# A hybrid decoder step on one core: the first norm moved behind its products, running sums taken on TensorE in split halves

## Chip, cores and metric

The kernel runs on one core of a Trainium2 chip. The metric is the device time of one execution in microseconds (us), lower is better, given as the median of several runs.

## The reference, cut to what matters

One step of a two-layer decoder is applied to 1024 prompt tokens and 8 sample tokens (1032 columns in all), with a model width of 1024. Only the start of the even layer is touched by the change:

```
hp = rmsnorm(xp, g_mix[l])                       # x * rsqrt(mean(x*x)+eps) * g
rq, rk, rv, rg, sq, sk, sv = split(h @ w_in)     # 28 tiles of 128 output features
# stick-breaking attention, per head of sq, sk, sv:
z = q @ k.T * hd**-0.5 + bias
log_1m = where(mask, log_sigmoid(-z), 0)         # -softplus(z)
after = reverse_cumsum(log_1m) - log_1m
a = where(mask, exp(log_sigmoid(z) + after), 0);  out = a @ v
# retention, per head: q, k = rotary(rq), rotary(rk); chunks of 128 tokens
ret_out = silu(rg) * head_layernorm(o, gn_g)
```

## The kernel before

Activations lie with features on the 128 partitions and the 1032 tokens in the free dimension: `X` has eight chunks of 128x1032. A product is run in full precision as three one-pass matmuls on rounded halves (`three`, line 435): `Wh*Hh + Wh*Hl + Wl*Hh`, each in three groups of 344 columns, so one chunk of the contraction is nine matmuls (`chunk`, L439) and a tile of 128 output features is eight chunks. GpSimd splits each 512 KB weight tile into `Wh` and `Wl` (L410, L412) when the tile two before it is done. SyncE queues the loads.

**Start.** SyncE loads the first quarter of x (1032 KB, two chunks), the constants (778 KB), the parameters (356 KB), the selectors (32 KB), the rest of x, then the weights. ScalarE squares each chunk, VectorE sums the squares (L1298 `acc`), TensorE adds over the partitions (`norm_sum`, L502), ScalarE takes the root, VectorE the reciprocal of all 1032 columns (L1326), and only then VectorE forms each normalised chunk `hf`, ScalarE its high half and VectorE its low half. The products wait for these. `first_pair` (line 468) runs two tiles together: chunks 0 to 3 of the first, then chunk k of the first beside chunk k-4 of the second. A third tile follows; ScalarE evacuates all three from PSUM.

Later norms are already in a deferred form (`DEFERRED`): the halves are made of x times its gain, the sum of squares runs beside the products (`high_of_x`, `low_of_x`, `group_sum` L465, `roots`, `reciprocals` L1378), and the reciprocal root is multiplied in where the product is evacuated.

**Stick-breaking, four heads.** The scores of a head are cut into 12 units of a key block of 128 and up to 512 queries; the widths are 128, 256, 384, 512, 512, 512, 512, 512, then 128, 256, 384, 512. Units go in pairs, six groups g per head. In each group TensorE runs, in this order: two score products of the next pair (L537), two chunks of the next head's products, the sums of the first unit (L547, L551), one chunk, the sums of the second unit, one chunk, the value products of the pair before (L560). So 24 chunks, three tiles, are spread over a head. Per unit VectorE scales the scores out of PSUM (L1409), ScalarE takes Abs, Exp and Ln, VectorE makes the softplus `sp`, and the cumulative sum over keys is two fp32 matmuls: a triangle times `sp`, and ones times a running sum `rr` that VectorE keeps (`later`, two buffers, cleared by a memset). VectorE subtracts the sum from the score (`exponent`), ScalarE takes Exp (`aa`). Banks 3 and 4 of PSUM hold scores, bank 5 the sums, 6 and 7 the values. ScalarE evacuates the next head's three tiles (`next_product`).

**Retention, four heads.** The tile of the gate `rg` is evacuated with Silu; rotary rows `cs` are loaded when stick-breaking has ended; the cached pages of the samples are streamed through two buffers by SyncE, each released by its consumer. The values are transposed and copied to `vt` by ScalarE. At the end of a head VectorE takes a reciprocal, and ScalarE evacuates the next gate after the last product with the old one (`r_c`).

Of the kernel before, what the change touches and what calls it, by code (L numbers as in the profile page):

```python
# [90 lines left out]
def build(nc, x_in, mem_in, wts, memw, cons, rope, selc, par, stc, stf0, stf1, stret,  # L91
          cache_k, cache_v, cmk, cmv, ptab,
          y, o_sbk, o_sbv, o_retp, o_rets, o_cvp, o_cvs, o_ffn0, o_ffn1, o_st0, o_st1, o_mk, o_mv):
    with ExitStack() as ctx:
# [25 lines left out]
        def sem(name):  # L120
# [26 lines left out]
        DEFERRED = (1, 2, 4, 5)  # L147
        n_at = [sum(3 if k in DEFERRED else 1 for k in range(nk)) for nk in range(7)]
        hf_at = {0: 0, 3: KC, 6: 2 * KC}
# [11 lines left out]
        rt, _ = layout([("cs", [P, 2, N]), ("rg", [P, N]),  # L161
# [8 lines left out]
        rt.update(layout([("rst", [P, N])], where["kt"])[0])  # L170

# [113 lines left out]
        LATER = {u: n for n, u in enumerate(u for u, (_, j, _, _) in enumerate(UNITS) if j)}  # L285
        NLATER = len(LATER)

# [6 lines left out]
        def _(sp):  # L294
# [26 lines left out]
            load_x(0)  # L321
            load(con[:, :], cons, ld_con)
            load(prm[:, :], par, ld_con)
            load(sel[:, :, :], selc, ld_con)
            for c in range(1, KC // 2):
                load_x(c)
            for j in range(2):
                weight(j, j, first=True)
            weights(2, T_RET + 6)

            ended(sp, E_SB)
            load(rt["cs"][:, :, :], rope, ss("ld_rope"))
# [68 lines left out]
        def _(pool):  # L401
# [13 lines left out]
            pool.wait_ge(ld_con, 48)  # L415
# [16 lines left out]
        def _(pe):  # L432
# [26 lines left out]
            def group_sum(nk, g):  # L459

                if g < 2:
                    pe.wait_ge(ss("n_acc"), KC * (nk + 1))
                else:
                    pe.wait_ge(ss("n_rt"), n_at[nk] + 1)
                mm(ps[:, 6 + g % 2, 0:GN], ones, dn["acc_d"][:, g * GN:(g + 1) * GN], start=True,  # L465
                   stop=True).then_inc(ss("n_sum"), 1)

            def first_pair(t, ready, freed=None, act_h=HA, nk=None):
# [44 lines left out]
            pe.wait_ge(ld_con, 48)  # L513
            norm_sum(0)

            first_pair(T_SB, split_ready(0))
            pe.wait_ge(ss("sb_ev"), 1)
            tile(T_SB + 2, 0, 0)
            for i in range(0, 2):
                for hh in range(2):  # L520
# [3 lines left out]
                    pe.wait_ge(ss("sb_ev"), 3 * h + 3)  # L524
                    if hh:
# [14 lines left out]
                    def sums(u):  # L540

                        half, j, q0, w = UNITS[u]
                        lone = j == 4 * half + 3
                        pe.wait_ge(ss("sb_sp"), NU * h + (u + 1))
                        if u >= 1 or hh:
# [385 lines left out]
        def _(act):  # L931
# [11 lines left out]
            def fixed():  # L943

                act.wait_ge(ld_con, 48)
# [21 lines left out]
            def high_of_x(nk, freed, gcol, act_h):  # L967

                for c in range(KC):
                    act.wait_ge(set_free[c % 2], freed + c // 2 + 2)  # L970
# [5 lines left out]
            def roots(nk):  # L976

                for g in range(GRP):
                    act.wait_ge(ss("n_sum"), n_at[nk] + g + 1)
                    fn(dn["rst_d"][:, g * GN:(g + 1) * GN], ps[:, 6 + g % 2, 0:GN], ACT.Sqrt, ss("n_rt"),  # L980
                       scale=1.0 / D, bias=eps)

            act.wait_ge(ld_con, 48)
            for c in range(KC):
                act.wait_ge(ld_x[c // 2], 16)
                square(0, c)
            norm(0)

            def sb_evacuate(j, hh, s, done):

                act.wait_ge(tile_done, done)
                fn(grp(sb[f"{'kvq'[j]}{hh}"][:, :]), pset(s), ACT.Copy, ss("sb_ev"))

            for j in range(3):
                sb_evacuate(j, 0, j % 2, T_SB + j + 1)
            for i in range(0, 2):
                for hh in range(2):
# [7 lines left out]
                    def front(g):  # L1005

                        for u in (2 * g, 2 * g + 1):
                            w = UNITS[u][3]
                            act.wait_ge(ss("sb_zs"), NU * h + (u + 1))
                            if u >= 4 or hh:  # L1010
                                act.wait_ge(ss("sb_sp"), NU * h + (u - 3))
# [1080 lines left out]
```

## Time and profile before

| | us |
|---|---|
| median of 3 runs | 3418.16 (3417.29 to 3421.23) |
| the profiled execution, its own time | 3422.02 |
| its span, first to last instruction | 3420.2 |
| PE busy in the span | 3210.9 (94%) |
| DVE busy | 1859.5 (54%) |
| ACT busy | 748.5 (22%) |
| POOL busy | 788.6 (23%) |

The engines are PE (TensorE matmuls), PEld (weight loads into TensorE), DVE (VectorE), ACT (ScalarE), POOL (GpSimd) and SP (SyncE). Busy shares are over the whole span; what counts for the change is the first fifth of it, up to about 683 us.

### The profile page before, as it was taken

How to read it: one execution, taken by the hardware profiler on the slowest of the kernel's cores; microseconds unless marked ns; L12 is line 12 of the kernel's file. 1: busy time of each engine (PE TensorE's matmuls, PEld its weight loads, DVE VectorE, ACT ScalarE, POOL GpSimd, SP SyncE). 2: the span in 40 equal slices, each digit the busy share in tenths (PEclk: the TensorE clock that was granted, in tenths of full speed). 3: DMA queues.
4: the chain of work that ended last, by engine and by line, in shares of the span. 5: the costliest groups of instructions: out<-in, count | busy, mean ns of one | idle time of the engine just before them, and what ended most of it. 6: DMA issues, size and time to landing. Idle time of an engine off the chain costs nothing.

```text
span 3420.2 us, 45029 instructions
## 1 busy us (share of the span) xinstructions
PE 3210.9 (94%) x19126; PEld 2953.8 (86%) x19126; DVE 1859.5 (54%) x2789; ACT 748.5 (22%) x1029; POOL 788.6 (23%) x424
## 2 busy tenths in 40 slices
PE   5999999499989999999998899799999999999996
PEld 4777888399769999999998788499679999999996
DVE  5444565643434654455546799852345554555456
ACT  3656222220031211111112322320032211111111
POOL 2111211033004233333333000123003332323331
PEclk9999999699999999999999999899999999999998
DMA  3011344422701111111112010012701111111111
GB/s 119 32 38 38 106 145 154 130 99 73 295 28 48 50 44 50 44 50 44 50 44 62 25 37 26 26 38 75 320 7 48 50 44 50 44 50 44 50 44 69
DMA packets 83643, 238.16 MB, mean 70 GB/s; under 512 B 15722, under 2 KB 20714, under 8 KB 81522
## 3 DMA queue, kind: packets, MB, share of 16 engines
q1 hardware_dynamic: 74962, 217.96, 19.4%
q10 hardware_dynamic: 8480, 17.32, 1.4%
q8 instruction: 151, 2.47, 0.3%
q14 instruction: 50, 0.41, 0.0%
HBM read 217.93 MB, written 17.32 MB: 69 GB/s over the span
## 4 chain that ended last, share of the span: by engine, by line
PE 85%; DVE 9%; DMA 2%; ACT 1%; issue 1%; SPq 1%; ACTq 0%; DVEq 0%
PE ps L439 69%; PE ps L897 2%; PE ps L815 2%; PE ps L738 2%; PE ps L726 2%; PE ps L792 1%; DVE tls L1306 1%; DVE X L1298 1%; DMA pg<-in_cv 1%; PE ps L560 1%; PE ps L547 1%; PE ps L551 1%; PE ps L537 1%; PE ps L502 1%; DVE Gl L1298 1%
## 5 line engine op out<-in xcount | busy, mean ns | idle before, releaser
L439 PE MATMUL ps<-Hh,Wh 128*128 128x344 f32 x3552 | 792.3, 332 | 53.3 <-DVE Hl L1298 45.4
L410 POOL CAST Wh<-wraw 128x1024 fp32r<-128x1024 f32 x210 | 233.4, 1111 | 2565.0 <-PE ps L439 2531.9
L439 PE MATMUL ps<-Hl,Wh 128*128 128x344 f32 x3552 | 758.4, 322 | 0.0
L439 PE MATMUL ps<-Hh,Wl 128*128 128x344 f32 x3552 | 754.8, 321 | 0.0
L439 PEld LDWEIGHTS ps<-Hh,Wh 128*128 128x128 f32 x3552 | 604.0, 190 | 92.6 <-issue 75.8
L439 PEld LDWEIGHTS ps<-Hl,Wh 128*128 128x128 f32 x3552 | 605.6, 190 | 0.0
L439 PEld LDWEIGHTS ps<-Hh,Wl 128*128 128x128 f32 x3552 | 596.8, 189 | 0.0
L412 POOL TENSOR_TENSOR Wl<-wraw,Wh 128x1024 fp32r<-128x1024 f32 x210 | 555.1, 2643 | 16.8
L1298 DVE TENSOR_TENSOR X<-ps,X 128x1032 f32<-128x1032 f32 x200 | 244.4, 1230 | 296.6 <-PE ps L439 296.6
L1298 DVE TENSOR_TENSOR ub<-ps,rst_d 128x1032 f32<-128x1032 f32 x88 | 108.5, 1233 | 424.8 <-PE ps L439 241.7
L1302 DVE SCALAR_TENSOR_TENSOR cb<-ub,fp,cb 128x1024 f32<-128x1024 f32 x176 | 275.7, 1566 | 93.4 <-ACT cb L939 93.4
L939 ACT ACTIVATE cb<-ub,fp 128x1032 f32<-128x1032 f32 x88 | 110.1, 1252 | 967.5 <-DVE ub L1298 967.5
L439 PE MATMUL ps<-Gh,Wh 128*128 128x344 f32 x1056 | 225.7, 322 | 4.0 <-DVE X L1298 4.0
L439 PE MATMUL ps<-Gl,Wh 128*128 128x344 f32 x1056 | 224.2, 320 | 0.0
L439 PE MATMUL ps<-Gh,Wl 128*128 128x344 f32 x1056 | 224.2, 320 | 0.0
L439 PEld LDWEIGHTS ps<-Gh,Wh 128*128 128x128 f32 x1056 | 176.3, 188 | 9.7 <-DVE X L1298 9.7
L439 PEld LDWEIGHTS ps<-Gl,Wh 128*128 128x128 f32 x1056 | 178.2, 188 | 0.0
L439 PEld LDWEIGHTS ps<-Gh,Wl 128*128 128x128 f32 x1056 | 177.2, 188 | 0.0
L439 PE MATMUL ps<-Hh_s,Wh 128*128 128x344 f32 x768 | 164.7, 323 | 0.0
L439 PE MATMUL ps<-Hl_s,Wh 128*128 128x344 f32 x768 | 162.8, 320 | 0.0
L439 PE MATMUL ps<-Hh_s,Wl 128*128 128x344 f32 x768 | 162.1, 319 | 0.0
L1302 DVE SCALAR_TENSOR_TENSOR ca<-uu,cpar,ca 128x512 f32<-128x512 f32 (+1 forms) x232 | 155.0, 744 | 0.0
(234 smaller groups left out, 3320.1 us busy)
## 6 DMA issues: line engine op xcount, KB each, us to landing
wraw<-in_wts SPq DMA_DIRECT2D x224, 512.0 KB, 3.5
pg<-in_ck SPq DMA_DIRECT2D x64, 256.0 KB, 2.8
pg<-in_cv SPq DMA_DIRECT2D x64, 256.0 KB, 2.8
cc<-in_cmk SPq DMA_DIRECT2D x16, 1024.0 KB, 9.8
cc<-in_cmv SPq DMA_DIRECT2D x16, 1024.0 KB, 9.6
X<-in_x SPq DMA_DIRECT2D x8, 1032.0 KB, 7.2
mwa<-in_memw SPq DMA_DIRECT2D x16, 512.0 KB, 7.5
mwb<-in_memw SPq DMA_DIRECT2D x16, 512.0 KB, 7.6
```

Of the source, the lines that this page charges most:

```text
L410: pool.tensor_copy(Wh[:, j, :], wraw[:, j, :]).then_inc(w_hi, 1)
L412: pool.tensor_tensor(Wl[:, j, :], wraw[:, j, :], Wh[:, j, :].bitcast(F32), ALU.subtract).then_inc(w_split, 1)
L439: ins = mm(o, w[:, wcol[0], wcol[1]:wcol[1] + P], r, start=first and a == 0, stop=last and a == 2)
L502: ins = mm(ps[:, 3 * s + g, 0:GN], ones, src[:, g * GN:(g + 1) * GN], start=True, stop=True)
L537: mm(ps[:, 3 + u % 2, 0:w], k_[:, j * P:(j + 1) * P], q[:, q0:q0 + w], start=True, stop=True).then_inc(ss("sb_z"), 1)
L726: ins = mm(ps[:, mk_bank(c), 0:MEM], mws[c % 4][:, k * P:(k + 1) * P], nmem["memT"][:, k, :], start=k == 0, stop=k == KC - 1)
L738: ins = mm(ps[:, 6 - 2 * half + m, :], nmem["memT"][:, 2 * kk + k, m * P:(m + 1) * P], mws[t % 4][:, k * 512:(k + 1) * 512], start=(kk == ...
L815: ins = mm(ps[:, 6 + dc, :], cr["mv"][:, m, (2 * hx + dc) * P:(2 * hx + dc + 1) * P], at["pT"][:, u % 2, m, :], start=m == 0, stop=m == MT ...
L897: ins = mm(ps[:, 6 + c % 2, :], cf["dg"][:, n, :], cf["us2"][:, n:n + TH], start=n == 0, stop=n == W_PE - 1)
L939: ins = act.activation(out, in_, f, **kw)
L1298: ins = dve.tensor_tensor(out, a, b, op)
L1302: ins = dve.scalar_tensor_tensor(out=out, in0=in0, scalar=scalar, in1=in1, op0=op0, op1=op1)
```

## The change

Three things are altered. The first norm takes the deferred form: products run on x times its gain, and the reciprocal root `rst0` (kept where chunk 3 of x was) is multiplied in at each evacuation, which moves from ScalarE to VectorE. For retention it is multiplied into the rotary rows once, inside head 1, into the values by a per-token scale (`rtok`, made by nine one-column matmuls), and into the gate by VectorE before Silu. The loads are put in another order, in pieces of one, two, two and three chunks, each weight between them. And the running sum `rr` goes: PSUM bank 5 keeps the sum across units, to which each unit adds its own triangle (`own`), after the rest of the unit before (`next`, ones minus triangle), each in two one-pass matmuls on the high and low half of the softplus, with three slots for the halves.

```
-        DEFERRED = (1, 2, 4, 5)
+        DEFERRED = (0, 1, 2, 4, 5)
...
-                        ("sp", [P, 2, 512]), ("rr", [P, 2, 512]), ("ea", [P, 4, 512]),
-                        ("aa", [P, 2, 512])], hd_end)
+                        ("sph", [P, 3, 512], F32R), ("spl", [P, 3, 512], F32R),
+                        ("ea", [P, 4, 512]), ("aa", [P, 2, 512]),
+                        ("own", [P, P], F32R), ("next", [P, P], F32R)], hd_end)
...
+        rst0 = C[:, 3, :]
+        rope0 = C[:, 0:2, :]
...
# SyncE
+            first_x(0, 0, 1)
+            load(prm[:, :], par, ss("ld_rope"))
+            weight(0, 0, first=True)
+            first_x(1, 1, 3)
+            weight(1, 1, first=True)
+            first_x(2, 3, 5)
+            first_x(3, 5, KC)
             load(con[:, :], cons, ld_con)
             load(sel[:, :, :], selc, ld_con)
+            weights(2, 4)
+            sp.wait_ge(ss("n_acc"), KC)
+            load(rope0, rope, ss("ld_rope"))
+            weights(4, T_RET + 6)
             ended(sp, E_SB)
-            load(rt["cs"][:, :, :], rope, ss("ld_rope"))
...
# TensorE
-                    if nk in DEFERRED and k == 5:
+                    if nk in DEFERRED and k == (5 if nk else KC):
                         group_sum(nk, 0)
                         group_sum(nk, 1)
-                    if nk in DEFERRED and k == 7:
+                    if nk in DEFERRED and k == (7 if nk else KC + 1):
                         group_sum(nk, 2)
...
+                    if h == 0:
+                        for c in range(TT):
+                            mm(ps[:, 5, c:c + 1], rst0[:, c * P:(c + 1) * P], ident[:, 0:1], start=True, stop=True)
+                        mm(ps[0:NS, 5, TT:TT + 1], rst0[:, T:N], ident[:, 0:1], start=True,
+                           stop=True).then_inc(ss("r_tok"), 1)
...
-                        ins = mm(ps[:, 5, 0:w], tri, sb["sp"][:, u % 2, 0:w], start=True, stop=lone)
-                        if not lone:
-                            pe.wait_ge(ss("sb_rr"), NLATER * h + LATER[u - 1] + 1)
-                            ins = mm(ps[:, 5, 0:w], ones, sb["rr"][:, u % 2, q0 - 512 * half:512],
-                                     start=False, stop=True)
+                        if not first:
+                            before = UNITS[u - 1][3]
+                            for part in ("sph", "spl"):
+                                mm(ps[:, 5, 512 - before:512], sb["next"][:, :], sb[part][:, (u - 1) % 3, 0:before],
+                                   start=False, stop=False, skip_group_check=True)
+                        pe.wait_ge(ss("sb_lo"), NU * h + (u + 1))
+                        for part in ("sph", "spl"):
...
+                            ins = mm(ps[:, 5, 512 - w:512], sb["own"][:, :], sb[part][:, u % 3, 0:w],
+                                     start=first and part == "sph", stop=j == 0 and part == "spl",
+                                     skip_group_check=True)
...
# ScalarE
+                        act.wait_ge(ld_x[(c + 1) // 2 if c < 6 else 3], 16)
...
+                    def high(u):
+                        w = UNITS[u][3]
+                        act.wait_ge(ss("sb_sp"), NU * h + (u + 1))
+                        if u >= 3 or hh:
+                            act.wait_ge(ss("sb_s"), NU * h + max(u - 1, 0))
+                        fn(sb["sph"][:, u % 3, 0:w], sb["lg"][:, u % 4, 0:w], ACT.Copy, ss("sb_hi"))
...
                             fn(sb["lg"][:, u % 4, 0:w], sb["zs"][:, u % 4, 0:w], ACT.Abs, ss("sb_sp1"))
+                            between(u - 2)
...
-                        if g in (2, 4):
-                            next_product(g // 2 - 1)
                         if g + 1 < NU // 2:
-                            front(g + 1)
+                            front(g + 1, high)
...
+                for c in range(TT):
+                    fn(rt["vt"][:, c, :], ps[:, 6 + c // 4, (c % 4) * P:(c % 4 + 1) * P], ACT.Copy,
+                       ss("r_vt") if c % 4 == 3 else None, scale=rtok[:, c:c + 1])
+                if i == 0:
+                    fn(rt["cs"][:, :, :], rope0, ACT.Copy, ss("r_tok"))
...
                     fn(grp(rt["rst"][:, :]), pset(1), ACT.Sqrt, ss("r_root"), scale=1.0 / P, bias=eps)
+                    act.wait_ge(ss("r_g"), 2 * i + 1)
+                    fn(rt["rg"][:, :], rt["rg"][:, :], ACT.Silu, ss("r_g"))
...
# VectorE
+                tt_(grp(sb[f"{'kvq'[j]}{hh}"][:, :]), pset(s), grp(rst0), ALU.mult, ss("sb_ev"))
...
+                    def low(u):
+                        w = UNITS[u][3]
+                        dve.wait_ge(ss("sb_hi"), NU * h + (u + 1))
+                        tt_(sb["spl"][:, u % 3, 0:w], sb["lg"][:, u % 4, 0:w],
+                            sb["sph"][:, u % 3, 0:w].bitcast(F32), ALU.subtract, ss("sb_lo"))
...
+                        if h == 1 and g in (1, 3):
+                            dve.wait_ge(ss("ld_rope"), 32)
+                            tt_(rope0[:, g // 2, :], rope0[:, g // 2, :], rst0, ALU.mult, None)
+                        if g in (2, 4):
...
+                            next_product(g // 2 - 1)
...
                         softplus(2 * g)
-                        later(2 * g)
                         softplus(2 * g + 1)
+                        low(2 * g)
+                        low(2 * g + 1)
                         exponent(2 * g)
-                        later(2 * g + 1)
                         exponent(2 * g + 1)
+                    next_product(2)
...
                 def deviation():
+                    tt_(rt["rg"][:, :], rt["rg"][:, :], rst0, ALU.mult, ss("r_g"))
```

## Rows read from the trace of the kernel before

**Rows 1.** The page: shares of the chain that ended last, by engine.
```profile
PE 85%; DVE 9%; DMA 2%; ACT 1%; issue 1%; SPq 1%; ACTq 0%; DVEq 0%
```
**Rows 2.** Windows: busy time by stage; columns named in the first line.
```profile
core 0: us, PE busy (x) PEld busy (x) DVE busy (x) ACT busy (x) POOL busy (x), PEclk, DMA share, GB/s
0.00:38.70 38.70, 3.78 (x6) 1.88 (x7) 24.67 (x16) 14.21 (x13) 8.77 (x8) 1.00 0.51 194
38.70:78.30 39.60, 36.78 (x216) 35.68 (x216) 15.76 (x14) 9.50 (x9) 7.85 (x5) 1.00 0.09 27
78.30:359.10 280.80, 265.58 (x1265) 204.20 (x1266) 127.36 (x244) 168.89 (x253) 43.20 (x26) 1.00 0.12 38
```
**Rows 3.** Timeline of the start: start us, us, engine, line, operation, idle before.
```profile
11.37 2.21 ACT L939 ACTIVATE sq<-X 128x1032 f32<-128x1032 f32 x2 [0.36 <-DMA X<-in_x]
...
17.73 1.04 POOL L410 CAST Wh<-wraw 128x1024 fp32r<-128x1024 f32 x1 [17.28 <-DMA wraw<-in_wts]
38.70 1.20 PE L439 MATMUL ps<-Hh,Wh 128*128 128x344 f32 x3 [11.63 <-DVE Hl L1298]
77.22 1.03 ACT L939 ACTIVATE q<-ps 128x1032 f32<-128x1032 f32 x1 [10.32 <-PE ps L439]
```
**Rows 4.** Groups by form, one tile (min/median/max ns), and a timeline row: deferred norms.
```profile
L1302 DVE SCALAR_TENSOR_TENSOR Hl<-X,prm,Hh 128x1032 fp32r<-128x1032 f32 x16 | 20.5, 1284 | 0.0
L939 ACT ACTIVATE Hh<-X,prm 128x1032 fp32r<-128x1032 f32 x16 | 18.6, 1161 | 112.5 <-DVE X L1298 112.5
...
L1298 DVE TENSOR_TENSOR acc_d<-acc_d,rst_d x28: 1220/3426/3446, 724.6 to 2639.7; 128x1032 f32<-128x1032 f32 x28
...
788.77 4.46 DVE L1378 RECIPROCAL rst_d<-rst_d 128x344 f32<-128x344 f32 x2 [1.52 <-ACT rst_d L939]
```
**Rows 5.** Chain of waits in head 2 and retention's first head: start us, us, what.
```profile
249.62 0.86 PE ps L547 x2
...
251.34 1.43 PE ps L439 x9
...
421.27 1.70 PE ps L657 x16
```
**Rows 6.** What PE waited for, 78.3 to 359.1 us: total, times, longest.
```profile
PE ps L537 <- DVE zs L1298: 5.2, 4, 1.3
PE ps L560 <- ACT aa L939: 3.5, 4, 0.9
```
**Rows 7.** Groups by form, 78.3 to 359.1 us: busy, mean ns; idle before.
```profile
L939 ACT ACT_TABLE_LOAD x49 | 62.9, 1283 | 0.9
L939 ACT ACTIVATE aa<-ea 128x512 f32<-128x512 f32 x24 | 14.0, 615 | 0.0
...
L1409 DVE TENSOR_SCALAR zs<-ps,prm 128x512 f32<-128x512 f32 x24 | 18.0, 749 | 17.3 <-PE ps L537 16.4
L1298 DVE TENSOR_TENSOR ea<-zs,ps 128x512 f32<-128x512 f32 x24 | 16.5, 689 | 47.9 <-PE ps L551 47.9
```
**Rows 8.** Timeline of ACT in head 2, a table load and its successor.
```profile
226.96 1.28 ACT L939 ACT_TABLE_LOAD   x1
228.26 1.04 ACT L939 ACTIVATE lg<-lg 128x384 f32<-128x384 f32 x2
```
**Rows 9.** Timelines of POOL and DVE in head 2, a weight split beside softplus.
```profile
242.52 2.38 POOL L412 TENSOR_TENSOR Wl<-wraw,Wh 128x1024 fp32r<-128x1024 f32 x1
...
244.35 1.10 DVE L1302 SCALAR_TENSOR_TENSOR sp<-zs,lg 128x512 f32<-128x512 f32 x1
```
**Rows 10.** Timelines of DVE and ACT at the end of retention's first head.
```profile
427.32 1.23 DVE L1302 SCALAR_TENSOR_TENSOR t<-ps,t 128x1032 f32<-128x1032 f32 x1 [3.61 <-PE ps L502]
439.32 6.60 DVE L1602 RECIPROCAL rst<-rst 128x1032 f32<-128x1032 f32 x1 [10.77 <-ACT rst L939]
447.28 1.95 DVE L1298 TENSOR_TENSOR C<-t,rg 128x1032 f32<-128x1032 f32 x1
...
450.10 1.03 ACT L939 ACTIVATE rg<-ps 128x1032 f32<-128x1032 f32 x1
```

More of the change, by code:

```diff
@@ L170, in build, with rst_of @@
         rt.update(layout([("rst", [P, N])], where["kt"])[0])
+        rtok, _ = place("rtok", [P, TT + 1], F32, rt_end)
+        rst0 = C[:, 3, :]
+        rope0 = C[:, 0:2, :]
+        def rst_of(nk):
+            return dn["rst_d"][:, :] if nk else rst0
         rt["sm"], rt["qd"] = (rt[x][:, 0:T].rearrange("p (c n) -> p c n", c=TT) for x in ("t1", "t2"))
@@ L319, in load_x, with first_x @@
                 load(X[:, 2 * c:2 * c + 2, :], x_in[:, 2 * c:2 * c + 2, :], ld_x[c])
-            load_x(0)
+            def first_x(s, c0, c1):
+                load(X[:, c0:c1, :], x_in[:, c0:c1, :], ld_x[s])
+            first_x(0, 0, 1)
[5 more added lines that the diff above has]
+            first_x(3, 5, KC)
             load(con[:, :], cons, ld_con)
-            load(prm[:, :], par, ld_con)
             load(sel[:, :, :], selc, ld_con)
[L325 to L329, printed above, removed]
+            weights(2, 4)
+            sp.wait_ge(ss("n_acc"), KC)
+            load(rope0, rope, ss("ld_rope"))
+            weights(4, T_RET + 6)
             ended(sp, E_SB)
-            load(rt["cs"][:, :, :], rope, ss("ld_rope"))
             load(rt["pt"][:, :], ptab, ss("ld_pt"))
@@ L979, in roots @@
                     act.wait_ge(ss("n_sum"), n_at[nk] + g + 1)
-                    fn(dn["rst_d"][:, g * GN:(g + 1) * GN], ps[:, 6 + g % 2, 0:GN], ACT.Sqrt, ss("n_rt"),
+                    fn(rst_of(nk)[:, g * GN:(g + 1) * GN], ps[:, 6 + g % 2, 0:GN], ACT.Sqrt, ss("n_rt"),
                        scale=1.0 / D, bias=eps)
[L983 to L995, printed above, removed]
+            act.wait_ge(ss("zeroed"), 1)
+            fn(dn["gap"][:, 0:8], selr[:, 0, 0:8].bitcast(F32), ACT.Square, None)
+            act.wait_ge(ss("ld_rope"), 16)
+            high_of_x(0, None, PCOL["g_mix"], HA)
+            act.wait_ge(ld_con, 32)
+            roots(0)
             for i in range(0, 2):
@@ L1056, in evacuate @@
                 act.wait_ge(tile_done, done)
-                fn(grp(rt[("rk", "rvT", "rq", "rg")[j]][:, :]), pset(0), ACT.Silu if j == 3 else ACT.Copy,
-                   ss("r_ev"))
+                fn(grp(rt[("rk", "rvT", "rq", "rg")[j]][:, :]), pset(0), ACT.Copy, ss("r_ev"))
             def head(i, more):
@@ L1369, in add_to_x @@
                     if c:
[L1370 to L1371 removed]
+                        low_of_x(c - 1, nk, gcol, act_h)
+                low_of_x(KC - 1, nk, gcol, act_h)
             def reciprocals(nk):
@@ L1384, in _, with sb_evacuate @@
                 copy(selr[a:a + NS, :, :], sel[:, :, :], None)
-            for c in range(KC):
-                sum_square(0, c)
-            norm(0, PCOL["g_mix"])
+            reciprocals(0)
+            def sb_evacuate(j, hh, s, done):
+                dve.wait_ge(tile_done, done)
+                tt_(grp(sb[f"{'kvq'[j]}{hh}"][:, :]), pset(s), grp(rst0), ALU.mult, ss("sb_ev"))
+            dve.wait_ge(ss("n_rc"), 3)
+            for j in range(3):
+                sb_evacuate(j, 0, j % 2, T_SB + j + 1)
+            dve.wait_ge(ss("r_tok"), 1)
+            copy(rtok[:, 0:TT], ps[:, 5, 0:TT], None)
+            copy(rtok[0:NS, TT:TT + 1], ps[0:NS, 5, TT:TT + 1], ss("r_tok"))
+            fixed()
+            copy(sb["own"][:, :], tri, None)
+            tt_(sb["next"][:, :], ones, tri, ALU.subtract, ss("sb_own"))
             for i in range(0, 2):
```

136 lines of the change are left out of this document (67 added, 69 removed).

## Prediction

> **What bounds the kernel now.** The chain of work that ended last, read first, is 85% TensorE [rows 1]. A share over the whole span says nothing of the first fifth, which is all that the change touches, so the windows come next [rows 2]. The start divides at 38.7 us: before it TensorE works 3.8 us of 38.7, after it 36.8 of 39.6. So 35 us pass before the first product, and the timeline tells why [rows 3]: its first matmul at 38.70 waited 11.63 us for VectorE's low half, the last link of square, sum, root, reciprocal and scaling. The weights landed at 17.73, well before. Stick-breaking, 78.3 to 359.1, is the other kind: TensorE is busy 265.6 of 280.8 us and ACT 168.9, DVE 127.4. Its own waits list [rows 6] holds 5.2 us for scores and 3.5 for the last values, a few us in four heads. There, what is taken off TensorE shortens the time until another engine can't keep up.
>
> **The start, step by step.** Between the quarter of x at 11.37 and the first weights at 17.73 came two quarters and 512 KB, 2576 KB in 6.36 us, 405 KB per us [rows 3]. By 11.37 the queue had moved 3230 KB. In the new order the sums are 516 KB (first chunk), 872 (parameters), 1384 (weight 0), 2416 (chunks 1, 2), 2928 (weight 1), 3960 (chunks 3, 4), 5508 (the rest). At that rate they land at 4.7, 5.5, 6.8, 9.4, 10.6, 13.2 and 17.0 us. The high half takes 1.16 and the low half 1.28 [rows 4]: chunk 0 is ready at 8.0. The split of weight 0 (cast 1.04 [rows 3], subtraction 2.38 [rows 9]) ends about 10.3, so TensorE starts there instead of 38.7. Chunk 1 is ready at 11.9. From then VectorE sets the pace with 1.28 for a low half and 1.22, the shortest of the sums [rows 4], 2.50 per chunk: chunk 7 at 26.9. The median sum however took 3.43, not 1.22 [rows 4]. That length goes with POOL's weight subtraction beside it, and weight 1 is subtracted at just that time; one such meeting adds 2.2.
>
> TensorE needs 1.43 for a chunk of nine matmuls [rows 5]. From chunk 4 two tiles run together, 2.86 per step against 2.50, so it is the slower one: four steps from 21.9 (19.4 + 2.2, and a hand-over) end at 33.3. Three partition sums of 344 columns cost 1.7 (0.86 for 512 [rows 5]), the other four chunks 5.7: 40.7. The third tile must wait for its PSUM set: first sum at 33.9, root 0.8 (under the 1.03 of 1032 columns [rows 3]), three reciprocals at 2.23 (4.46 for two [rows 4]), evacuation about 1.23 on VectorE: 42.7. Eight chunks to 54.1, evacuation to 55.3. Before, the same point was 77.22 + 1.03 = 78.25 [rows 3]. **The start gives 23.0 us**; without the meeting 25.
>
> The rotary load, now behind the last sum, stands ahead of weight 4 on SP's queue: 1032 KB, 2.5 us. Weight 4 can't be loaded before weight 2 is split, which waits for the first tile at about 32, and it is needed after 54. Covered; if it weren't, 2.5.
>
> **Stick-breaking.** A four-byte matmul of 512 columns takes 0.86, 1.68 ns a column; a half's matmul 1.43 / 9 / 344 = 0.46 ns [rows 5]. The widths add up to 4608 per head. Before: triangle 4608 and ones 4352 (not for the first unit of each half), 8960 columns, 15.05 us. After: own 4608 and next 3584 (the width of the unit before), both halves, 16384 columns, 7.55 us. That removes 7.5 per head, **30.0 in four**. Against it:
> - nine one-column matmuls on the root: eight such took 1.70 [rows 5], so 1.9, once, in front of head 0; VectorE's copies behind them and the two small tiles are about 1, beside TensorE's transposes;
> - the first unit of a head gets two hand-overs more, ScalarE's high half and VectorE's low half, while TensorE has nothing else left: from 0 (the memset that goes gives it back) to 1.3 (two steps and the second softplus); I take 0.6, 2.4 in four;
> - before the last values TensorE idles 0.88 per head [rows 6], partly because ScalarE still evacuates there; of this 2.0 comes back (0 to 3.5);
> - softplus beside a weight split took 1.10 [rows 9] where other two-input operations of 512 columns take 0.69 [rows 7]; twelve groups have a split: 0 to 4.9, I take 1.0, since VectorE has slack.
>
> Sum **-26.7**. The cover: a wide group on TensorE is now four chunks 5.7, four four-byte matmuls 3.4, eight half matmuls 1.9, 11.0; a mean one 9.7. The loop beside it is exponent to exponent: two scores 1.5, two softplus 1.4, Abs and high half 1.2, low half 0.7, exponent 0.7, second sums 1.1, exponent 0.7 [rows 7], 7.3. It fits, with 2.4 to spare. ACT loses three evacuations (3.1) and gains twelve copies (6.1, at 0.615 for 512 columns): 45.2 per head from 42.2, of 63.5. DVE gains three evacuations (3.7), its low halves replace the running sums and the memsets: about 36 per head. The two products with the rotary rows in head 1 (2.5) stand where VectorE waits for scores. Without these covers each costs what is given.
>
> Here a rule would make it otherwise. Table loads took 1.28 each, 12 to a head [rows 7], and the next operation began 1.30 after the start of the load [rows 8].
> The Trainium skill (ScalarE: Activation LUTs, section What ACT_TABLE_LOAD costs) gives 1.28 for the load and 1.38 more of drain. The row has no room for the second part, so the sum goes by 1.28; by 2.66 ACT would reach 61.8 per head (estimate), see the rivals.
>
> **Retention.** The gate's evacuation at a head's end, at 450.10, stood behind a load of Silu's table; its operand was free at 449.2 [rows 10]. As a copy it starts 0.85 earlier, in three heads: **-2.4** (0 to -3). Silu and its load, 2.3, move beside VectorE's reciprocal of 6.60; the gate's product with the root, 1.2, into VectorE's wait of 3.61 [rows 10]. The eight small copies for `vt` (one ACT operation for four, some 1.2 more) and the copy of the rotary rows (2) are followed by a whole tile of TensorE before anything is due. Without these covers, 1 to 2 per head.
>
> **Sum.** -23.0 - 26.7 - 2.4 = -52.1. The profiled execution took 3422.0, so 3369.9; the median of the runs is 3.9 below it: **3366**.
>
> **Rivals.**
> 1. The loop takes TensorE's place in part of the groups: the added copy and subtraction meet locks and late scores. For it: four VectorE steps with two inputs and ACT at 70%. Against: 2.4 spare per group. If half of the stage's gain goes: 3379.
> 2. The start gives half. TensorE is fed in bursts, and after its long idle the first three matmuls took 1.20 [rows 3] where nine take 1.43; with chunks at twice the time while two tiles run together, four steps cost 11.4 more: 3377. Against: in the second window [rows 2] the 24 chunks came in such bursts too and fitted into 39.6 us, which at twice the time would be 68.6.
> 3. Slower: the loop from softplus over ScalarE's copy to the low half sets every group of stick-breaking. It decides from 12.8 us a group: (280.8 + 25.4) / 24. At 13.2 the stage takes 317, and the whole +11: 3429. The loop's 7.3 with all four two-input steps held 2.2 would still be 16, so it isn't excluded; but a split runs in half of the groups and for 2.4 us only.
> 4. The one-pass form doesn't work for these tiles and each half costs a four-byte matmul: 27.5 per head instead of 15.05, +50, in all about +28: 3446. Against: all products on split halves run at 0.46 ns.
> 5. The table drain. ACT at 61.8 per head would set the pace with some 67 per head, 268 for the stage: gain 13, 3379. Rows 8 speak against it.
> 6. No change: the loop eats the stage's gain and the start is held up by more: within 7 us of 3418.
>
> **How the numbers follow.** Forecast 0.66, its own range 3358 (every bound on the good side: 25, 31.6 and 3) to 3380 (start 20.5, stage 18, nothing in retention); rival 1 0.14, rival 2 0.11, rival 3 0.03, rival 4 0.02, rival 5 0.02, rival 6 0.02. A measurement can tell about 0.2%, 7 us, from no change. Faster: forecast and rivals 1, 2, 5: 0.93. Slower: 3 and 4: 0.05. Same: 0.02. The range runs from 3354 (that 3358 less the 4 by which the runs spread) to 3390, which takes in rivals 1, 2 and 5 with 10 of spread.
>
> **What would show it.** First product near 10 us, head 0's transposes near 57 rather than 78; the low halves 2.5 apart with one of 3.4 among the sums. Stick-breaking: heads of 63 to 64 us, TensorE's share as before, sums of a wide unit about 0.95 long, no list of waits of TensorE for low halves beyond the first unit. Retention: heads shorter by 0.8, no table load before the gate's evacuation. The forecast is wrong if TensorE waits for low halves in every group, or if the first tile's evacuation comes later than about 45.

## The result, and the profile after

The changed kernel takes **3374.75 us** (median of 4 runs, 3370.11 to 3381.17) against 3419.69 of the kernel before beside it: a ratio of 0.9867, 95% interval 0.9854 to 0.988, so 45 us less. The forecast was 3366, with a range from 3354 to 3390. The profiled execution took 3373.28 (span 3371.4); against the profile of before the span is shorter by 48.8.

The chain of work that ended last, by engine, is the one of before [rows 1] with hardly a figure changed. At this level the profile doesn't show that anything happened.

```profile
PE 85%; DVE 10%; DMA 2%; ACT 2%; issue 1%; SPq 0%; DVEq 0%; ACTq 0%
```

The windows do. This is stick-breaking in the changed kernel; the columns are those of [rows 2].

```profile
61.80:314.20 252.40, 238.41 (x1267) 199.41 (x1266) 144.70 (x262) 177.86 (x289) 40.97 (x25) 1.00 0.13 41
```

Stick-breaking takes 252.4 us and not 280.8, and TensorE now begins at 11.3 us and not at 38.7 (first row of the start, below). Against the forecast, by the two profiled executions (each stage ends where the next begins):

| Stage | before | after | gain | forecast |
|---|---|---|---|---|
| start, to the query's evacuation | 78.25 | 59.7 | 18.5 | 23.0 |
| stick-breaking, with the nine root columns | 280.8 | 254.5 | 26.4 | 26.7 |
| retention, to the first output product | 326.3 | 323.6 | 2.7 | 2.4 |
| the rest | 2734.86 | 2733.63 | 1.2 | 0 |
| span | 3420.2 | 3371.4 | 48.8 | 52.1 |

The medians differ by 45.0, 3.8 less than the profiled executions do: the one of before lay 2.3 above its median, the one of after 1.5 below its own.

**The start.** TensorE in the start (start us, us, engine, line, operation; in brackets the idle time before and what ended it):

```profile
11.34 1.23 PE L450 MATMUL ps<-Hh,Wh 128*128 128x344 f32 x3 [11.34 <-POOL Wl L424]
...
34.65 1.32 PE L478 MATMUL ps<-acc_d,con 128*128 128x344 f32 x4
...
45.29 0.74 PE L450 MATMUL ps<-Hh,Wh 128*128 128x344 f32 x3 [2.83 <-DVE k L1326]
45.87 0.68 PE L450 MATMUL ps<-Hl,Wh 128*128 128x344 f32 x3
46.34 1.07 PE L450 MATMUL ps<-Hh,Wl 128*128 128x344 f32 x3
47.20 1.07 PE L450 MATMUL ps<-Hh,Wh 128*128 128x344 f32 x3
...
59.77 1.95 PE L537 MATMUL ps<-con,C 128*128 128x1 f32 x16 [1.32 <-DVE q L1326]
```

VectorE, GpSimd and ScalarE beside it:

```profile
9.00 2.83 DVE L1334 COPY acc_d<-rst_d 128x1032 f32<-128x1032 f32 x1
...
12.81 3.24 POOL L424 TENSOR_TENSOR Wl<-wraw,Wh 128x1024 fp32r<-128x1024 f32 x1
...
13.74 3.40 DVE L1326 TENSOR_TENSOR acc_d<-acc_d,rst_d 128x1032 f32<-128x1032 f32 x1
...
18.27 1.23 DVE L1326 TENSOR_TENSOR acc_d<-acc_d,rst_d 128x1032 f32<-128x1032 f32 x1
...
21.78 1.28 DVE L1330 SCALAR_TENSOR_TENSOR Hl<-X,prm,Hh 128x1032 fp32r<-128x1032 f32 x1
...
35.47 1.28 ACT L961 ACT_TABLE_LOAD   x1 [5.40 <-PE ps L478]
...
37.34 6.62 DVE L1406 RECIPROCAL C<-C 128x344 f32<-128x344 f32 x3 [4.72 <-ACT C L961]
```

Read it backwards from 59.77. The third tile started at 45.29, 2.6 later than the forecast's 42.7, and lasted 13.2 instead of 11.4, because four of its triples of matmuls, in its first two chunks, came 0.86 us apart (from 46.34 to 49.77), where the others come 0.47 apart. It waited 2.83 us for the key's evacuation, which stood behind three reciprocals, these behind a load of Sqrt's table, that behind TensorE's sums at 34.65. The granted clock of the third tile's two parts, in the same columns as above:

```profile
46.34:49.70 3.36, 3.36 (x14) 3.36 (x13) 0.04 (x1) 0.00 (x0) 0.00 (x0) 0.50 0.53 156
49.80:58.40 8.60, 8.60 (x55) 8.36 (x54) 0.00 (x0) 0.00 (x0) 0.00 (x0) 1.00 0.01 2
```

0.50 is the lower of the clock's two levels, 1.2 GHz. TensorE had waited 2.83 us just before.

**Stick-breaking.** Where TensorE waited, 61 to 314 us (total, times, longest), to lay beside [rows 6]:

```profile
PE ps L552 <- DVE zs L1326: 5.2, 4, 1.3
...
PE ps L572 <- issue: 1.5, 1, 1.5
...
PE ps L582 <- ACT aa L961: 1.0, 4, 0.3
```

The wait for the scores is the same; that for the last values fell from 3.5 to 1.0. No row names a low half, but the row of 1.5 under "issue" is a wait for one. It stands before the first sums of head 0:

```profile
71.03 0.30 PE L572 MATMUL ps<-sph,own 128*128 128x128 f32 x1 [1.53 <-issue]
```

VectorE's low half of that unit ended at 70.92, 0.11 us earlier; in experiment 9 the list names the low half for the same place. In the kernel before, TensorE waited 0.45 there. The heads begin at 61.77, 125.93, 188.71 and 251.41, and the stage ends at 314.19: 64.2 (with that wait) and three times 62.7, against 71.0 and three times 69.9 of before. The chain in head 2 (start us, us, what), with the sums of a 128-column unit first and of two wide ones behind:

```profile
196.47 0.44 PE ps L572 x2
...
214.73 0.67 PE ps L572 x2
...
216.82 0.46 PE ps L566 x2
217.28 0.47 PE ps L572 x2
```

The two wide pairs at 216.82 sum to 0.93 (forecast 0.95), where a wide unit took 0.86 for each of two products [rows 5].

**Retention.** What TensorE waited for at the beginning of a head's first product fell from 6.6 to 4.1 us in three heads (the kernel before first):

```profile
PE ps L610 <- ACTq L257: 6.6, 3, 2.2
...
PE ps L632 <- ACTq L266: 4.1, 3, 1.6
```

### The profile page after: what moved, and what is told of

Read it like the earlier page. It is cut to its first block, busy times and chain, and to the rows that moved or that the text cites. A ratio compares the mean times of both kernels' runs of the same rounds, so it can differ in the third digit from the quotient of the medians.

```text
span 3371.4 us, 45117 instructions
## 1 busy us (share of the span) xinstructions
PE 3184.4 (94%) x19144; PEld 2952.0 (88%) x19144; DVE 1892.9 (56%) x2808; ACT 764.0 (23%) x1093; POOL 789.1 (23%) x424
## 4 chain that ended last, share of the span: by engine, by line
PE 85%; DVE 10%; DMA 2%; ACT 2%; issue 1%; SPq 0%; DVEq 0%; ACTq 0%
PE ps L450 69%; PE ps L919 2%; PE ps L837 2%; PE ps L760 2%; PE ps L748 2%; PE ps L814 1%; DVE tls L1334 1%; DVE X L1326 1%; PE ps L582 1%; DVE t L1326 1%; PE ps L552 1%; DVE junk L1559 1%; DVE Gl L1326 1%; PE ps L515 1%; DMA pg<-in_cv 1%
## 5 line engine op out<-in xcount | busy, mean ns | idle before, releaser
L450 PE MATMUL ps<-Hh,Wh 128*128 128x344 f32 x3552 | 779.3, 328 | 55.2 <-DVE Hl L1326 30.9
```

Of the source, the lines that this page charges most:

```text
L450: ins = mm(o, w[:, wcol[0], wcol[1]:wcol[1] + P], r, start=first and a == 0, stop=last and a == 2)
```

## The experiments

Runs of one program spread here by up to 11 us (3370.11 to 3381.17), so an experiment in the start or in retention is read by its stage in the profile. Differences of medians are against 3374.75.

**1. The key's evacuation early.** ScalarE copies the first tile out; VectorE multiplies in SBUF later.

```
             act.wait_ge(ld_con, 32)
+            act.wait_ge(tile_done, T_SB + 1)
+            fn(grp(sb["k0"][:, :]), pset(0), ACT.Copy, ss("sb_ev"))
             roots(0)
...
-            for j in range(3):
+            dve.wait_ge(ss("sb_ev"), 1)
+            tt_(sb["k0"][:, :], sb["k0"][:, :], rst0, ALU.mult, None)
+            for j in range(1, 3):
                 sb_evacuate(j, 0, j % 2, T_SB + j + 1)
```

> The changed kernel, but the first tile (the key of head 0) is copied out of PSUM by ScalarE as soon as it is done, before the roots, and VectorE multiplies it by the reciprocal root afterwards in SBUF. Theory: the third tile waits 2.83 us for that PSUM set, and its first chunks run at half pace because TensorE idled; with the set free early there is no idle time, the third tile starts near 42.3 instead of 45.29 and runs 1.43 per chunk from the start, so the query is evacuated near 54.9 instead of 59.7: 4.8 us earlier. Rival: the half pace has another cause than the idle time and stays; then 3.0 us earlier. Rival: weight 2's split or something else holds the third tile: 0 to 1 us.

TensorE of this kernel, across the place where it had waited:

```profile
41.55 0.63 PE L450 MATMUL ps<-Hh,Wl 128*128 128x344 f32 x3
42.02 0.64 PE L450 MATMUL ps<-Hh,Wh 128*128 128x344 f32 x3
...
54.87 1.95 PE L537 MATMUL ps<-con,C 128*128 128x1 f32 x16 [1.33 <-DVE q L1328]
```

No wait, no slow triple in the third tile, and the root columns start 4.9 us earlier (54.87 against 59.77), as the theory had it. One run of 3368.59.

**2. Matmuls in the gap.**

```
+            pe.wait_ge(ss("n_rt"), 3)
+            for n in range(5):
+                mm(ps[:, 6 + n % 2, 0:GN], ones, dn["acc_d"][:, 0:GN], start=True, stop=True)
             pe.wait_ge(ss("sb_ev"), 1)
             tile(T_SB + 2, 0, 0)
```

> The changed kernel with five extra matmuls of 344 four-byte columns into PSUM banks that nobody reads, in the idle time before the third tile (about 2.9 us of work that adds nothing to any output). Theory: the third tile still starts near 45.3, but at 0.48 us per three matmuls instead of 0.86 in its first 4.5 us, so the query is evacuated 1.8 us earlier. Rival: the half pace doesn't come from the idle time; then the same time to 0.2 us, or later if the extra matmuls run long.

```profile
41.99 3.05 PE L529 MATMUL ps<-acc_d,con 128*128 128x344 f32 x10
44.98 0.74 PE L450 MATMUL ps<-Hh,Wh 128*128 128x344 f32 x3
...
57.92 2.10 PE L540 MATMUL ps<-con,C 128*128 128x1 f32 x16 [1.33 <-DVE q L1329]
```

The third tile waits as long for its PSUM set and starts at 44.98, but the root columns come 12.94 us later and not 14.48: work that nobody reads made the useful work 1.5 us shorter. So the half pace came from the wait. The Trainium skill (TensorE: Matmul & The Clock Gate, section What's actually happening) says that the engine is throttled by default and that activity releases it; these rows agree, 0.50 granted in the slow stretch above, and here 1.00 from 45 to 56.4 and no slow triple. The run took 3376.91, within the spread.

**3. x in pairs of chunks.**

```
-            first_x(0, 0, 1)
+            first_x(0, 0, 2)
...
-            first_x(1, 1, 3)
+            first_x(1, 2, 4)
...
```

> The changed kernel with x loaded in pairs of chunks: chunk 0 no longer alone, but with chunk 1 (1032 KB before the parameters and weight 0 instead of 516). Theory: VectorE sets the pace from its first low half on, so its whole chain and the query's evacuation come later by the time of 516 KB at 405 KB per us: 1.3 us. Rival: the chunks that follow come early enough and the meetings of VectorE with GpSimd's splits fall otherwise: between 1 us earlier and no change.

VectorE's first low half, and TensorE's third tile:

```profile
7.87 2.16 DVE L1330 SCALAR_TENSOR_TENSOR Hl<-X,prm,Hh 128x1032 fp32r<-128x1032 f32 x1 [5.93 <-ACT Hh L961]
...
46.27 1.23 PE L450 MATMUL ps<-Hh,Wh 128*128 128x344 f32 x3 [2.83 <-DVE k L1326]
```

Both are later than in the changed kernel (6.93, 45.29) by 0.9 and 1.0. By these two marks the first chunk alone is worth 1 us, the theory's direction at less than its 1.3. The query's evacuation, by which the theory had measured it, came 2.2 later: the root columns start at 61.95, because the third tile behind its gap had seven slow triples here and not four, 1.2 us more. In the run's time, 3372.99, it can't be seen.

**4. The first square straight into the sum.** VectorE's copy at 9.00 goes.

```
+                    if not nk and c == 0:
+                        fn(dn["acc_d"][:, :], X[:, c, :], ACT.Square, ss("n_acc"))
+                        continue
```

> The changed kernel with the square of chunk 0 written by ScalarE straight into the sum, so that VectorE's copy (2.83 us, beside GpSimd's subtraction) goes. Theory: VectorE is what feeds TensorE until chunk 4, so chunk 1's low half starts near 10.6 instead of 11.76 and the low half of chunk 4 ends at least 1.1 us earlier than 23.06; the query's evacuation comes 1.1 to 3.4 us earlier, the more the fewer meetings are left. Rival: the next VectorE operation meets GpSimd's subtraction in its place and nothing is gained: 0 to 0.5 us.

VectorE and GpSimd of this kernel:

```profile
13.06 3.24 POOL L424 TENSOR_TENSOR Wl<-wraw,Wh 128x1024 fp32r<-128x1024 f32 x1
...
13.99 3.41 DVE L1333 SCALAR_TENSOR_TENSOR Hl<-X,prm,Hh 128x1032 fp32r<-128x1032 f32 x1
...
20.82 1.29 DVE L1333 SCALAR_TENSOR_TENSOR Hl<-X,prm,Hh 128x1032 fp32r<-128x1032 f32 x1
```

Chunk 4's low half ends at 22.11 instead of 23.06, and the root columns start at 58.73 instead of 59.77: 1.0 us, just under the theory's range and above the rival's. The reason is the rival's: a copy of 2.83 went, but other operations met the subtractions. A low half took 3.41 beside it, where the sum had taken 3.40 and each alone takes 1.23 to 1.29. The Trainium skill (SBUF — State Buffer, section Who interferes with whom) says that a VectorE instruction with two SBUF inputs contends with a GpSimd instruction that reads SBUF, over a shared port pair that is an exclusive lock. Both rows agree: VectorE's operation, begun second, ends 1.1 us after the subtraction (17.40 and 16.30 here, 17.14 and 16.05 in the changed kernel), about its own length alone. The meeting doesn't belong to one instruction but to 3 us of time.

**5. Two slots of halves instead of three.**

```
-                        if u >= 3 or hh:
-                            act.wait_ge(ss("sb_s"), NU * h + max(u - 1, 0))
+                        if u >= 2 or hh:
+                            act.wait_ge(ss("sb_s"), NU * h + u)
...
```

> The changed kernel with two slots of softplus halves instead of three. ScalarE's copy of an odd unit must then wait until the sums of the even unit before it are done, since these read the slot. Theory: a chain takes the place of the one chunk between the two sums of a group: copy 0.62, low half 0.69, exponent 0.69 and hand-overs, 2.4 us for a wide unit against 1.43 of TensorE; 0.6 to 1.0 us more in each of 24 groups, +14 to +24 us against the changed kernel, in TensorE's waits for low halves or exponents. Rival: the halves are ready long before and the third slot does nothing: 0 to +3 us.

Measured 3395.35 (3393.91 to 3396.2), ratio to before 0.9929 (0.9913 to 0.9946): 20.6 us slower than the changed kernel. The heads take 66.6 instead of 62.7; the stage is 16.7 longer (269.1 against 252.4), inside the theory's 14 to 24. About 1 of it isn't the slot's: three heads are 3.9 longer each, and head 0, where the granted clock was 0.50 from 61.4 to 71.5, is 4.9 longer. The rest of the difference lies outside the stage; this profiled start was 2.0 later, with seven slow triples in the third tile and root columns at the lower clock. TensorE's waits in the stage have a new first row:

```profile
PE ps L566 <- DVE ea L1326: 10.0, 16, 0.7
```

ScalarE and TensorE in a wide group of head 2 show the chain link by link:

```profile
226.63 0.40 PE L572 MATMUL ps<-spl,own 128*128 128x512 f32 x1
...
227.12 0.63 ACT L961 ACTIVATE sph<-lg 128x512 fp32r<-128x512 f32 x1 [1.09 <-PE ps L572]
...
229.13 0.50 PE L566 MATMUL ps<-sph,next 128*128 128x512 f32 x1 [0.70 <-DVE ea L1326]
```

ScalarE starts its copy when the even unit's sums end, and the odd unit's start 2.1 us later, with one chunk between. So the third slot carries about 16 of the stage's 26 us.

**6. The same sums on four-byte operands.** No halves; 'own' and 'next' on the softplus itself.

```
-                            for part in ("sph", "spl"):
-                                mm(ps[:, 5, 512 - before:512], sb["next"][:, :], sb[part][:, (u - 1) % 3, 0:before],
+                            mm(ps[:, 5, 512 - before:512], sb["next"][:, :], sb["lg"][:, (u - 1) % 6, 0:before],
...
-                            front(g + 1, high)
+                            front(g + 1)
...
```

> The changed kernel with the products 'own' and 'next' on the four-byte softplus itself (no halves, no copy on ScalarE, no low half on VectorE; six slots). Theory: the gain of stick-breaking comes from halves at 0.46 ns a column instead of 1.68: 8192 four-byte columns per head are 13.8 us against 7.5, +6.2 per head, less the two hand-overs of the first unit (0.6 per head): +22 us against the changed kernel, heads of about 68.5 us. Rival: the gain came from taking VectorE's running sums off the path, and the form of the product counts for little: 0 to +5 us.

Measured 3398.71 (3396.54 to 3403.35), ratio 0.9938 (0.9922 to 0.9955), 24.0 slower. The heads behind the first take 68.0 to 68.3, the stage 274.7, which is 22.3 more than with halves. TensorE is busy all through it (263.66 of 275.00):

```profile
61.00:336.00 275.00, 263.66 (x1270) 205.33 (x1270) 119.68 (x214) 157.14 (x241) 41.48 (x25) 0.99 0.12 38
```

This is the theory's 22. The form of the product is most of the gain: without it the new sums leave 280.8 - 274.7, 6 us, of which 2.5 is the wait for the last values.

**7, 8. ScalarE's copy twice, VectorE's low half twice.** The extra result goes into a tile that nobody reads.

```
+                        fn(sb["jk"][:, 0:w], sb["lg"][:, u % 4, 0:w], ACT.Copy, ss("jk"))
                         fn(sb["sph"][:, u % 3, 0:w], sb["lg"][:, u % 4, 0:w], ACT.Copy, ss("sb_hi"))
```

```
+                        tt_(sb["jk"][:, 0:w], sb["lg"][:, u % 4, 0:w],
+                            sb["sph"][:, u % 3, 0:w].bitcast(F32), ALU.subtract, ss("jk"))
                         tt_(sb["spl"][:, u % 3, 0:w], sb["lg"][:, u % 4, 0:w],
```

> The changed kernel with ScalarE's copy of each softplus unit done twice (the first into a tile that nobody reads): 0.5 us more on average in each of 12 units per head, 1.0 per group, in the loop from softplus to the low half. Theory: the loop has 2.4 us to spare in a group, so only the first unit of a head pays: +2 to +5 us in four heads. Rival: ScalarE's copy is on the loop that sets the group's time: +12 to +25 us.

> The changed kernel with VectorE's subtraction of each low half done twice (the first into a tile that nobody reads): 0.55 us more on average per unit, 1.1 per group, ahead of the exponents. Theory: inside the 2.4 us that the loop has to spare in a group, so only the first unit of a head pays: +3 to +6 us in four heads. Rival: VectorE's steps are the loop that sets the group's time: +13 to +26 us.

The copy twice: 3385.04 (3382.38 to 3389.4), ratio 0.9904 (0.9887 to 0.9921), 10.3 slower; its stage 261.6, 9.2 more. The low half twice: 3379.09 (3374.01 to 3385.52), ratio 0.9884 (0.9863 to 0.9905), 4.3 slower; its stage 259.4, 7.0 more. By their stages both lie between the theory and the rival. By the medians the second lies inside the theory's 3 to 6, and its interval overlaps that of the changed kernel, so here the stage decides. The waits in the stage of the first:

```profile
PE ps L572 <- DVE spl L1329: 3.9, 11, 0.5
```

and of the second:

```profile
PE ps L572 <- DVE spl L1326: 4.5, 11, 0.5
```

Eleven waits, not four: beside a head's first unit, the first units of its third and fourth group pay, so half of the 24 groups. (The listed waits are 3.9 of 9.2 and 4.5 of 7.0; TensorE's busy time grew by more than 4 as well, which was not followed further.) The changed kernel shows why there is so little room. VectorE in head 2 before the sums at 214.73, in the third group (scores and softplus stand where lines are left out):

```profile
209.08 1.23 DVE L1326 TENSOR_TENSOR k<-ps,C 128x1032 f32<-128x1032 f32 x1 [0.72 <-PE ps L450]
...
213.92 0.69 DVE L1326 TENSOR_TENSOR spl<-lg,sph 128x512 fp32r<-128x512 f32 x1
```

The evacuation of the next head's key, which the change moved to VectorE, stands ahead of scores, softplus and low half; this ends at 214.61, and TensorE's use of it starts at 214.73. In these groups the loop and TensorE end within 0.1 us of each other. In the fourth group no evacuation stands in front, and the room is as small (VectorE and TensorE):

```profile
220.93 0.35 DVE L1452 TENSOR_SCALAR zs<-ps,prm 128x128 f32<-128x128 f32 x1 [2.46 <-PE ps L552]
...
223.63 1.52 DVE L1326 TENSOR_TENSOR spl<-lg,sph 128x512 fp32r<-128x512 f32 x2
...
224.47 0.42 PE L572 MATMUL ps<-sph,own 128*128 128x512 f32 x1
```

The first of the two low halves ends at 224.32, 0.15 before its use. VectorE does have 2.46 us to spare, but it spends them waiting for the next pair's scores, which TensorE makes at the beginning of the same group and which stand ahead of softplus and low half in VectorE's queue. Work behind the scores can't use that time.

**9. The sums alone on the kernel before.** Its start, loads, evacuations on ScalarE and retention stay.

```
-                        ins = mm(ps[:, 5, 0:w], tri, sb["sp"][:, u % 2, 0:w], start=True, stop=lone)
...
+                        pe.wait_ge(ss("sb_lo"), NU * h + (u + 1))
+                        for part in ("sph", "spl"):
+                            ins = mm(ps[:, 5, 512 - w:512], sb["own"][:, :], sb[part][:, u % 3, 0:w],
...
```

> The kernel before with the new running sums alone: halves in three slots, the products 'own' and 'next', evacuations still on ScalarE, the first norm not deferred, loads and retention as before. Theory: the stage's gain doesn't depend on the start: -30.0 for the products, +2.4 for the first units, +1.0 for softplus, the tail wait not given back since ScalarE still evacuates: -26.6 us, about 3393. Rival: without the evacuations' move to VectorE ScalarE binds the loop and half of the gain goes: about 3406.

Measured 3391.33 (3389.66 to 3401.8), ratio 0.9927 (0.9908 to 0.9947): 27.5 below the 3418.8 beside it, and the stage 255.4 instead of 280.8, 25.4 less. The theory had 26.6, the rival half of it. The wait for the last values stands at its old 3.5, and the wait for a low half has its name here:

```profile
PE ps L566 <- ACT aa L945: 3.5, 4, 0.9
...
PE ps L556 <- DVE spl L1316: 1.7, 2, 1.6
```

So the sums don't need the evacuations' move, and that move is worth the 2.5 by which the first row falls in the changed kernel. What is left of the 45.0 us, 17.5, belongs to the rest of the change: its start, that move and retention.

**10, 11. A table load before the gate's evacuation.** Once with a Silu of one column, once with an Exp right before it.

```
+                    fn(jg[:, n:n + 1], one, ACT.Silu, None)
                 act.wait_ge(tile_done, done)
                 fn(grp(rt[("rk", "rvT", "rq", "rg")[j]][:, :]), pset(0), ACT.Copy, ss("r_ev"))
```

> The changed kernel with a Silu of one column ahead of the gate's evacuation in retention, so that the table load of 1.28 us and a short operation stand there again (and Silu later needs none of its own unless another table came between). Theory: the gate's evacuation starts 0.85 us or somewhat more later at each head's end and TensorE's next head with it: +2.6 to +4 us over the three heads with a successor. Rival: retention's shorter heads come from elsewhere and the load is hidden: 0.

> The changed kernel with an Exp of one column right before the gate's evacuation at the end of each retention head (its output is read by nobody), so that a table load of 1.28 us stands between the attended pages' output and that evacuation again, as in the kernel before. Theory: the evacuation of the gate comes 0.85 to 1.5 us later, and TensorE's wait at the start of the next head is 2.2 to 2.9 us instead of 1.4: +2.5 to +4.5 us in three heads. Rival: the wait is set by VectorE's last copies or the stage's end and not by the evacuation: 0 to +0.5.

The first told nothing: Silu's table was still there, so its operation took 0.20 and no load came. Its one run took 3379.30, within the spread.

```profile
404.25 0.20 ACT L962 ACTIVATE jg<-con 128x1 f32<-128x1 f32 x1 [0.51 <-DVE C L1331]
```

The second put the load there. ScalarE, and TensorE's wait in the whole of retention:

```profile
404.19 1.28 ACT L962 ACT_TABLE_LOAD   x1
```

```profile
PE ps L633 <- ACTq L267: 7.2, 3, 2.4
```

The wait rose from 4.1 to 7.2 in three heads, 3.1, as the theory had it. The time didn't show it: three heads took 237.0 us (326.25 to 563.25) against 238.5 of the changed kernel, and the run 3372.06. Other waits of the stage differ by more: four of TensorE's waits for VectorE (for `t`, `k`, `st` and `kt`) sum to 14.1 in this run and to 18.9 in the changed kernel. So the wait is shown, and its worth in the whole is not.

**12. A version that goes further.** The early key, and VectorE's low halves ahead of its sums; the squares wait in four tiles that are free until later. The first square goes straight into the sum, so VectorE's copy at 9.00 goes too, as in experiment 4.

```
+            for c in range(KC):
+                low_first(c)
+                if c >= 3:
+                    add_first(c - 2)
+            add_first(KC - 2)
+            add_first(KC - 1)
```

> The changed kernel with the key of head 0 copied out early by ScalarE, and with VectorE's low halves ahead of its sums of squares in the start: the squares go into four tiles that are free until later (the first straight into the sum), and the sum of chunk c is made after the low half of chunk c + 2. Theory: until chunk 4 TensorE is fed by VectorE, and after it TensorE is the slower one; with lows no longer behind the sums, chunk 4's low half ends near 18.8 us instead of 23.06, and everything behind moves with it: the query evacuated near 50.6, against 59.7 in the changed kernel and 54.9 with the early key alone; about 9 us in all against the changed kernel, 3366. Rival: the meetings with GpSimd's subtractions hold the low halves instead of the sums, and only 1 to 2 us come on top of the early key's 4.9: 3369.

Measured **3364.93** (5 runs, 3363.6 to 3375.15), ratio 0.9841 (0.9827 to 0.9855) to the kernel before, 9.8 us below the changed kernel; the two intervals touch at 0.9854 and 0.9855. VectorE's low halves of chunks 3 and 4, TensorE at the root columns:

```profile
14.36 3.08 DVE L1342 SCALAR_TENSOR_TENSOR Hl<-X,prm,Hh 128x1032 fp32r<-128x1032 f32 x1 [0.26 <-ACT Hh L966]
...
18.50 1.28 DVE L1342 SCALAR_TENSOR_TENSOR Hl<-X,prm,Hh 128x1032 fp32r<-128x1032 f32 x1
...
51.62 1.95 PE L542 MATMUL ps<-con,C 128*128 128x1 f32 x16 [1.32 <-DVE q L1338]
```

Chunk 4's low half ends at 19.78, against 23.06 and the 18.8 that was expected; chunk 3's stands before it, 3.08 long beside the second subtraction, where 1.28 had been counted. The root columns start 8.15 us earlier than in the changed kernel, 3.25 of them on top of the early key; how much of this the missing copy brings (1.0 by itself in experiment 4) and how much the order wasn't separated.

## Why the prediction was right, and where it was off

The two mechanisms were the right ones, and two of the three terms came out within half a microsecond.

- **Stick-breaking, -26.7 forecast, -26.4 measured.** Experiment 6 shows that the halves' price carries it, and experiment 9 that it needs nothing of the start. Inside the sum errors cancelled, so that it came this close is partly luck. The term of 30.0 was too large: TensorE's busy time in the stage fell by 27.2 (265.58 to 238.41). Part of the shortfall are hand-overs that the profile counts as busy. The first pair of a head, 128 columns twice, would be 0.12 us by columns; it took 0.44 (196.47), while a pair of the same width in the middle of the head, at 234.93, took 0.17. The pair behind the key's evacuation took 0.67 instead of 0.47 (214.73). Against that, the 2.4 for the first units' hand-overs was paid outside the busy time in head 0 alone, where TensorE waited 1.53 us instead of 0.45, and the last values gave back 2.5 for the 2.0 taken. The root columns took 2.0, forecast 1.9.
- **"It fits, with 2.4 to spare" was wrong**, though nothing hung on it. The 7.3 counted VectorE's and ScalarE's operations from exponent to exponent. It left out the evacuation that the change puts in front of them in one group out of three, and that VectorE must wait for TensorE's scores inside the group before softplus can follow. So the time to spare lies ahead of the scores, and between a low half and its use about 0.1 is left in half of the groups. Experiments 7 and 8 charged 9.2 and 7.0 us for work that should have cost 2 to 6. Rival 1 stood closer than its 0.14.
- **The start, -23.0 forecast, -18.5 measured**, is the step that failed; 4.4 us in three places. First, chunk 4 was forecast for 21.9 with one meeting of VectorE and GpSimd; four operations met a subtraction or a cast (at 6.93, 9.00, 11.76 and 13.74: 2.15, 2.83, 2.06 and 3.40 us long, where they take 1.28, 0.70, 1.28 and 1.23 alone), TensorE took it up at 23.2, and its sums came at 34.65 instead of 33.3: 1.3. Second, the root was put at 0.8 us; a load of Sqrt's table, 1.28, stood before it (35.47): 1.3. Third, the third tile was put at 1.43 for a chunk, and ran four triples of its first two at the lower clock's pace: 1.8. This last is rival 2's mechanism, in a place where neither it nor the forecast had it, and at a price of 1.8 instead of 11.4. Experiments 1 and 2 show its cause. The prediction's own sign of being wrong, a first tile evacuated later than about 45, stood on its edge: the key's evacuation ended at 45.23.
- **Rival 2's own place** shows it in part: parts of the first four chunks ran at half pace (0.86 a triple from 11.34, and again from 18.97), but it cost little there, since TensorE was waiting for VectorE's low halves anyway (2.04 us before 18.40, 0.35 before 20.76), and from 23.2 to the third tile no triple is slow.
- **Retention, -2.4 forecast, -2.7 measured**: the wait at the head of the next product fell by 2.5, and experiment 11 puts it back with a table load. That the stage's 2.7 is this 2.5 is likely and not shown, since its heads differ by as much between runs.
- **Rivals 4 and 5** fell: one pass costs 0.23 us for 512 columns (half of a pair's 0.47), and ScalarE's table loads, 49 of 1.28 as before [rows 7], set no pace. Rivals 3 and 6 fell with the stage's 252.4 and the time.

The table's last row, 1.2 us in the rest, has no part of the change in it and stays unexplained; it is below what a measurement can tell.

## What to carry to other kernels

Where a wait of TensorE is removed, look for the next one and for what the engine's clock does behind it: here a gap of 2.83 us cost 4.9. Count the spare time of a loop group by group, with everything that stands in its queue there, and ask at which place of the queue it lies; test it by doing one step twice. A sum over a group hid that half of them had none where it was needed. And when an engine feeds another, give it the feeding work first: low halves ahead of sums, with one copy less, brought 3.25 us.

## What the hardware showed that was not expected

- A copy of 1032 columns with one input met GpSimd's subtraction as well: 2.83 us at 9.00, where GpSimd subtracted from 8.07 for 3.21; the same copy took 0.70 in the kernel before, with GpSimd at rest (row below). The prediction had looked for such meetings among operations with two inputs alone.
- After the gap of 2.83 us the clock didn't fall at once: the triples at 45.29 and 45.87 kept the full pace, and the fall came at 46.34. In the run with two slots the same gap was followed by slow triples from the first on (45.03 to 51.17). The start of the slow stretch moves between runs of the same instructions, and its price here was 1.6 and 2.8 us.
- From 11.34 to 15.7 the triples came 0.86 apart while the clock's column for that stretch says 1.00. The trace's first clock entry begins at 15.6, just before the first triple that isn't slow (15.72, 0.63 long where the slow ones are 1.06), and a stretch without an entry is printed as 1.00. So the column says nothing there, and the triples are to be believed.

The copy in the kernel before:

```profile
10.39 0.70 DVE L1306 COPY acc<-sq 128x1032 f32<-128x1032 f32 x1
```
